# Summing the query squares together with the output squares of the gated DeltaNet heads, without a root and factors of their own

## What is computed

```
q_a = l2norm(q_a); k_a = l2norm(k_a)        # x * rsqrt(sum(x*x) + 1e-6), over the 128 of a head
q = q * dk ** -0.5
o = chunked gated delta rule(q, k, v, g, beta)
o_a = rms_norm(o_a, gdn_norm) * silu(z_a)   # o * rsqrt(mean(o*o) + 1e-6)
```

## Time and profile before

| | |
|---|---|
| median of three runs | 2443.24 us |
| span of the profiled execution, first to last instruction | 2435.2 us |
| what lies around the span (difference of the two) | 8.0 us |
| TensorE busy in the span | 2333.0 us (96%) |
| VectorE, ScalarE, GpSimd busy | 1191.3, 997.0, 1127.8 us |
| mean granted TensorE clock | 0.980 of full |
| one eight-tile pair | 88 us, six of them |

### The profile page before, as it was taken

The page is one execution under the profiler, slowest core; times in us unless marked ns, Lnnn a source line. Parts: engine busy times, 40 slices in busy tenths (PEclk is TensorE's granted clock), DMA queues, the critical chain, the costliest instruction groups (busy, mean ns, idle before and its releaser), DMA issues.

```text
span 2435.2 us, 30531 instructions
## 1 busy us (share of the span) xinstructions
PE 2333.0 (96%) x11700; PEld 1926.4 (79%) x11700; DVE 1191.3 (49%) x2356; ACT 997.0 (41%) x1925; POOL 1127.8 (46%) x824
## 2 busy tenths in 40 slices
PE   6999998999999999999989999989999999999997
PEld 5678887788878888888867888878887788888886
DVE  4677676644442344440147777675454423444302
ACT  5554444444542333332265355344555323333222
POOL 4364454344345555554443553552343555555542
PEclk9999999999999999999989999989999999999998
DMA  4211111122223333333322111101222333333332
GB/s 135 61 52 53 48 44 40 35 75 77 75 78 96 96 93 98 95 99 96 96 65 65 44 49 52 44 27 53 78 75 69 89 96 94 96 99 96 96 99 82
DMA packets 98497, 183.20 MB, mean 75 GB/s; under 512 B 10929, under 2 KB 11057, under 8 KB 98225
## 3 DMA queue, kind: packets, MB, share of 16 engines
q1 hardware_dynamic: 98352, 181.26, 26.2%
HBM read 179.12 MB, written 2.10 MB: 74 GB/s over the span
## 4 chain that ended last, share of the span: by engine, by line
PE 87%; DVE 7%; ACT 3%; issue 1%; POOL 0%; DMA 0%; SPq 0%; DVEq 0%; ACTq 0%
PE bank L1288 84%; PE bank L1354 2%; DVE conv_acc L834 1%; PE bank L1580 1%; ACT w_hi L505 1%; PE bank L1348 1%; DVE ob_lo L831 1%; DVE a_t L834 1%; DVE packed L1065 0%; DVE qk_t L834 0%; ACT oa_hi L516 0%; DMA vecs_all<-vecs 0%; DVE normalised L834 0%; DVE left L834 0%; DVE packed_rows L831 0%
## 5 line engine op out<-in xcount | busy, mean ns | idle before, releaser
L418 POOL TENSOR_TENSOR w_lo<-w_raw,w_hi 128x512 fp32r<-128x512 f32 x668 | 935.3, 1422 | 1206.8 <-ACT w_hi L505 1206.6
L1288 PE MATMUL bank<-xn_hi,w_hi 128*128 128x512 f32 x1936 | 784.2, 405 | 10.9 <-POOL w_lo L418 3.6
L1288 PE MATMUL bank<-xn_hi,w_lo 128*128 128x512 f32 x1936 | 784.2, 405 | 0.0
L1288 PE MATMUL bank<-xn_lo,w_hi 128*128 128x512 f32 x1936 | 779.7, 403 | 0.0
L505 ACT ACTIVATE w_hi<-w_raw 128x512 fp32r<-128x512 f32 x668 | 384.6, 623 | 739.5 <-PE bank L1288 733.4
L1288 PEld LDWEIGHTS bank<-xn_hi,w_hi 128*128 128x128 f32 x1936 | 369.2, 191 | 89.4 <-issue 8.5
L1288 PEld LDWEIGHTS bank<-xn_hi,w_lo 128*128 128x128 f32 x1936 | 369.9, 191 | 77.6 <-issue 7.3
L1288 PEld LDWEIGHTS bank<-xn_lo,w_hi 128*128 128x128 f32 x1936 | 369.1, 191 | 77.0 <-issue 4.1
L831 DVE TENSOR_TENSOR residual<-residual,bank 128x512 f32<-128x512 f32 x32 | 22.0, 686 | 259.4 <-PE bank L1288 259.2
L1288 PE MATMUL bank<-mid_hi,w_hi 128*128 128x512 f32 x352 | 136.9, 389 | 0.0
L1288 PE MATMUL bank<-mid_lo,w_hi 128*128 128x512 f32 x352 | 136.9, 389 | 0.0
(11 more groups left out here) (256 smaller groups left out, 3449.4 us busy)
## 6 DMA issues: line engine op xcount, KB each, us to landing
w_raw<-w_tiles SPq DMA_DIRECT2D x668, 256.0 KB, 2.6
residual<-x_t SPq DMA_DIRECT2D x4, 512.0 KB, 5.2
out_t<-normalised SPq DMA_DIRECT2D x8, 256.0 KB, 2.2
rope<-rope SPq DMA_DIRECT2D x1, 1024.0 KB, 10.0
mats<-mats SPq DMA_DIRECT2D x1, 704.0 KB, 7.6
vecs_all<-vecs SPq DMA_DIRECT2D x1, 133.0 KB, 7.5
```

What stands on the lines that cost most here:

```text
L418: nc.gpsimd.tensor_tensor(w_lo[j][:], w_raw[j][:], w_hi[j][:].bitcast(F32), ALU.subtract).then_inc(s_lo, 1)
L1288: return nc.tensor.matmul(out, lhsT, rhs, start=start, stop=stop)
```

## The change

The query squares are taken with a scale (sqrt(1e-6) times 128) and kept until the end of the pair; for that `sq_q` gets slots of its own, and two attention tiles move by 64 bytes. At the end VectorE adds them to the output squares (`om`), and the one chain of ones-products `oss` sums both. The stage `ss`, `varq`, the query's root, reciprocal, `fq`, `fq2`, `ox` and `orf` go. Since `ss` leaves `STAGES` and `FILL_WEIGHT`, the products of a pair are dealt out anew over the steps that are left, and for tile 0 the convolution's places are now written out by hand, too.

```diff
-        sq_q = per_head("sq_q", 5)
+        sq_q = per_head("sq_q", 18)
...
-        STAGES = (["kt", "gb", "ss", "vt", "kbT", "kk", "qk", "sub", "T0_"]
+        STAGES = (["kt", "gb", "vt", "kbT", "kk", "qk", "sub", "T0_"]
...
-        FILL_WEIGHT = {8: {"start": 4.5, "gb": 4, "ss": 1.5, "qk": 4.5, "sub": 7.3, "T0_": 0.5, "P3_": 0.6, "w": 0.8, "oss": 3},
-                       4: {"start": 4.5, "kt": 2, "gb": 4, "ss": 1.5, "qk": 4, "sub": 6, "w": 0.8, "oss": 3}}
+        FILL_WEIGHT = {8: {"start": 4.5, "gb": 4, "qk": 4.5, "sub": 7.3, "T0_": 0.5, "P3_": 0.6, "w": 0.8, "oss": 3},
+                       4: {"start": 4.5, "kt": 2, "gb": 4, "qk": 4, "sub": 6, "w": 0.8, "oss": 3}}
...
-                    spot = {1: ("kk", "kk", "qk", "sub", "T0_")}
+                    spot = {0: ("vt", "vt", "kbT", "kk", "kk"), 1: ("kk", "kk", "qk", "sub", "T0_")}
...
# ScalarE
-                    nc.scalar.activation(sq_q[s][:], q_f[s][:], ACT.Square)
+                    nc.scalar.activation(sq_q[s][:], q_f[s][:], ACT.Square, scale=EPS ** 0.5 * HD)
...
-                act.wait_ge(gdn_v.sem, gdn_v.after(t, "varq1"))
-                nc.scalar.activation(rinv[:, :, 0, :], rinv[:, :, 0, :], ACT.Sqrt)
...
# VectorE
-                for s in range(2):
-                    dve.wait_ge(gdn_p.sem, gdn_p.after(t, f"ss{s}"))
-                    V.tensor_scalar(rinv[:, s, 0, :], bz[s][:, :NC], 4 * EPS, None, ALU.add)
...
-                dve.wait_ge(gdn_a.sem, gdn_a.after(t, "sqrtq"))
-                V.reciprocal(rinv[:, :, 0, :], rinv[:, :, 0, :])
-                V.tensor_scalar(fq[:, 0], rinv[:, :, 0, :], HD ** -0.5, None, ALU.mult)
-                stt(fq[:, 1], fq[:, 0], 1.0 / HD, fq[:, 0], ALU.mult, ALU.mult)
...
                 for s in range(2):
+                    dve.wait_ge(gdn_a.sem, gdn_a.after(t, f"osq{s}"))
+                    tt_(o_sq[s][:], o_sq[s][:], sq_q[s][:], ALU.add).then_inc(gdn_v.step(f"om{s}"), 1)
+                for s in range(2):
                     dve.wait_ge(gdn_p.sem, gdn_p.after(t, f"oss{s}"))
-                    tt_(ocol[:, s, :], bx[s][:, :NC], fq[:, 1, s, :], ALU.mult)
-                V.tensor_scalar(ocol[:], ocol[:], EPS, None, ALU.add)
+                    V.tensor_scalar(ocol[:, s, :], bx[s][:, :NC], 1.0 / HD, 4 * EPS * EPS * HD, ALU.mult, ALU.add)
...
-                tt_(ocol[:], ocol[:], fq[:, 0], ALU.mult)
...
# TensorE
-                for s in range(2):
-                    pe.wait_ge(gdn_a.sem, gdn_a.after(t, f"sqq{s}"))
-                    for c in range(NC):
-                        last = mm(bz[s][:, c:c + 1], sq_q[s][:, c, :], ones[:, 0:1])
-                    last.then_inc(gdn_p.step(f"ss{s}"), 1)
-                d.issue(dense_after["ss"])
-
                 for s in range(2):
                     pe.wait_ge(front_v.sem, front_v.after(t, f"silu{4 * s}"))
-                    pe.wait_ge(gdn_v.sem, gdn_v.after(t, f"varq{s}"))
...
-                    pe.wait_ge(gdn_a.sem, gdn_a.after(t, f"osq{s}"))
+                    pe.wait_ge(gdn_v.sem, gdn_v.after(t, f"om{s}"))
```

More of the change, by code:

```diff
@@ L152, in hybrid_trunk @@
         fac = sb("fac", [2, 3, NC])
-        fq = sb("fq", [2, 2, NC])
         rinv = sb("rinv", [2, 2, NC])
@@ L223, in hybrid_trunk @@
                                       for j, n in enumerate(("dx0", "dxs", "dx1", "dxt", "rq", "rk")))
-        dv = sb("dv", [SEQ], at=slot(52))
-        d_tanh = sb("d_tanh", [SEQ], at=slot(53))
+        dv = sb("dv", [SEQ], at=slot(52) + 64)
+        d_tanh = sb("d_tanh", [SEQ], at=slot(53) + 64)
         sg0 = slot(14) + 64
@@ L327, in hybrid_trunk @@
         gdn_p = steps("gdn_pe", [m for st in STAGES for m in (["sub"] if st == "sub" else two(st))])
-        gdn_a = steps("gdn_act", two("ztanh", "sqq", "sqk") + ["sqrtk", "sqrtq"] + two("exp", "kbT", "eg", "T0_")
+        gdn_a = steps("gdn_act", two("ztanh", "sqq", "sqk") + ["sqrtk"] + two("exp", "kbT", "eg", "T0_")
                       + [m for L in LV for m in two(f"P{L}_", f"T{L}_")][:-2] + two("w", "osq", "o") + ["osqrt"])
-        gdn_v = steps("gdn_dve", ["hcol", "htot", "zact0", "zact1", "vark", "rinvk", "fac", "kb0", "kd0", "kb1", "kd1"] + two("varq", "ga", "vb")
-                      + ["rinvq", "fq", "fq2"] + two("at") + ["inv0", "red0", "red1", "row"] + two("qk") + [m for j in range(SB - 1) for m in (f"col{j}", f"inv{j + 1}")] + ["whole"] + two("i0_")
+        gdn_v = steps("gdn_dve", ["hcol", "htot", "zact0", "zact1", "vark", "rinvk", "fac", "kb0", "kd0", "kb1", "kd1"] + two("ga", "vb")
+                      + two("at") + ["inv0", "red0", "red1", "row"] + two("qk") + [m for j in range(SB - 1) for m in (f"col{j}", f"inv{j + 1}")] + ["whole"] + two("i0_")
                       + [m for L in LV for m in two(f"U{L}_")]
                       + [m for c in range(NC) for m in two(f"V{c}_", f"S{c}_")][:-2]
-                      + two("ox") + ["ovar", "orinv", "orf"] + two("ou", "og"))
+                      + two("om", "ovar") + ["orinv"] + two("ou", "og"))
         gdn_g = steps("gdn_pool", two("ds", "dg", "mt3_", "qd", "mt4_", "mt5_", "qm", "mt6_", "kbg"))
@@ L443, in mask @@
                         nc.gpsimd.tensor_tensor(mt[L % 2][s][:], a_t[s][:], mat4(M_LEVEL + L - FIRST), ALU.mult).then_inc(gdn_g.step(f"mt{L}_{s}"), 1)
-                stages("kt", "gb", "ss")
+                stages("kt", "gb")
                 for s in range(2):
@@ L622, in gdn @@
                     act.wait_ge(front_v.sem, front_v.after(t, f"silu{4 * s + 2}"))
-                    nc.scalar.activation(sq_q[s][:], q_f[s][:], ACT.Square).then_inc(gdn_a.step(f"sqq{s}"), 1)
+                    nc.scalar.activation(sq_q[s][:], q_f[s][:], ACT.Square, scale=EPS ** 0.5 * HD).then_inc(gdn_a.step(f"sqq{s}"), 1)
                 for s in range(2):
@@ L631, in gdn @@
                 stages("kt", "gb")
-                act.wait_ge(gdn_v.sem, gdn_v.after(t, "varq1"))
-                nc.scalar.activation(rinv[:, :, 0, :], rinv[:, :, 0, :], ACT.Sqrt).then_inc(gdn_a.step("sqrtq"), 1)
-                stages("ss")
                 for s in range(2):
@@ L669, in gdn @@
                 stages("oss")
-                act.wait_ge(gdn_v.sem, gdn_v.after(t, "ovar"))
+                act.wait_ge(gdn_v.sem, gdn_v.after(t, "ovar1"))
                 nc.scalar.activation(ocol[:], ocol[:], ACT.Sqrt).then_inc(gdn_a.step("osqrt"), 1)
@@ L1031, in gdn @@
                 for s in range(2):
-                    dve.wait_ge(gdn_p.sem, gdn_p.after(t, f"ss{s}"))
-                    V.tensor_scalar(rinv[:, s, 0, :], bz[s][:, :NC], 4 * EPS, None, ALU.add).then_inc(gdn_v.step(f"varq{s}"), 1)
-                for s in range(2):
                     dve.wait_ge(gdn_p.sem, gdn_p.after(t, f"gb{s}"))
@@ L1119, in gdn @@
                 for s in range(2):
+                    dve.wait_ge(gdn_a.sem, gdn_a.after(t, f"osq{s}"))
+                    tt_(o_sq[s][:], o_sq[s][:], sq_q[s][:], ALU.add).then_inc(gdn_v.step(f"om{s}"), 1)
+                for s in range(2):
                     dve.wait_ge(gdn_p.sem, gdn_p.after(t, f"oss{s}"))
-                    tt_(ocol[:, s, :], bx[s][:, :NC], fq[:, 1, s, :], ALU.mult).then_inc(gdn_v.step(f"ox{s}"), 1)
-                dve.wait_ge(gdn_v.sem, gdn_v.after(t, "ox1"))
-                V.tensor_scalar(ocol[:], ocol[:], EPS, None, ALU.add).then_inc(gdn_v.step("ovar"), 1)
+                    V.tensor_scalar(ocol[:, s, :], bx[s][:, :NC], 1.0 / HD, 4 * EPS * EPS * HD, ALU.mult, ALU.add).then_inc(gdn_v.step(f"ovar{s}"), 1)
                 stages("oss")
@@ L1126, in gdn @@
                 V.reciprocal(ocol[:], ocol[:]).then_inc(gdn_v.step("orinv"), 1)
-                dve.wait_ge(gdn_v.sem, gdn_v.after(t, "orinv"))
-                tt_(ocol[:], ocol[:], fq[:, 0], ALU.mult).then_inc(gdn_v.step("orf"), 1)
                 for s in range(2):
@@ L1556, in gdn @@
                     if s == 0:
-                        pe.wait_ge(gdn_v.sem, gdn_v.after(t, "orf"))
+                        pe.wait_ge(gdn_v.sem, gdn_v.after(t, "orinv"))
                     spread(by[s], ocol[:, s, :]).then_inc(gdn_p.step(f"obc{s}"), 1)
```

## The result

Before 2443.19 us, after **2454.15 us** median of four runs each beside one another (2442.96 to 2443.61, and 2449.73 to 2458.88); the ratio is 1.0052, interval 1.0035 to 1.0069. The change makes the kernel slower by about half a per cent. The forecast was 2459.4 with a range of 2441 to 2475. The runs of after lie in two groups: 2449.73 and 2449.81 us at a mean granted clock of 0.976, 2458.49 and 2458.88 at 0.973. The profiled execution is the longest of them (span 2456.8 for 2458.88 us). In every run, time and span differ by 2.0 to 2.1 us, so the 8.0 us taken ahead of the prediction for what lies around the span do not lie there: the span of 2435.2 belongs to an execution of before of some 2437.3 us. Beside the experiments before ran from 2434.92 to 2443.81 us, so that is one of its short executions.

What follows compares the result with a forecast made beforehand. TensorE is busy 96%, but VectorE, with ScalarE behind it, sets the pace from `sub` to `U3_`. Terms +10.8 (six pairs), +3.4 (clock at `kk`), +2.0 (4-tile pairs): +16.2 on span 2435.2, plus 8.0: 2459.4 us, range 2441 to 2475.

Steps and rivals of the forecast that it cites:

- Tile 1 one product too late, VectorE idle for what it saved: Ahead of `sub`: tile 1 ends at `qk`'s first product, so VectorE idles the 1.9 us it saved before `t0_1`.
- Wait at `sub` 3.7 us: TensorE's wait for `packed_rows` before `sub` in eight-tile pairs grows from 1.98 to 3.7 us as the trace counts it.
- The limit of 2.5: Sign against the forecast: it is wrong if the wait at `sub` stays under 2.5 us.
- pairs under 88: Sign against the forecast: it is wrong if the pairs take less than 88 us.
- the price of the fall after `sub`: Time lost when the clock falls after the wait at `sub`, in every pair: 1.7 us taken, 2.8 by the farthest row.
- Fall of the clock after it in two pairs, +3.4 us: After the new wait at `kk`: clock falls in two of six eight-tile pairs, 1.7 us each, bounds 0 to 10.2.
- The wait of 0.2: At `oss`, end of an eight-tile pair: TensorE waits 0.2 us for the squares of o and the new sums.
- Pairs with 4 tiles +1.0 each: `kk` starts at about 399.8, `inv` 0.9 us later, `sub` about 0.5 later, sums cost 0.4; bounds -1.5 and +2.5.
- the third rival: VectorE's new sums run slow beside a busy GpSimd: 14.4 us more, 2473.5 us; chance 0.08.
- the clock does not fall more than now: Rival: each eight-tile pair gives +0.1 us instead of +1.8, 4-tile pairs +2.0, total 2445.8 us; chance 0.15.
- TensorE's saving stays: Rival: 1.7 us come off in each of 8 pairs, 13.6 us, total 2429.6 us; chance 0.13.
- The added sums are slow: Rival: VectorE's sums before `oss`, slowed by GpSimd, end 1.0 and 1.8 us later; 2473.5 us; chance 0.08.

Runs made afterwards that it cites:

- run 2: The kernel before, norm as before, with only the new deal of the dense products (weight of `ss` 0, tile 0's places as in the change); 2455.28 us, ratio 1.0049.
- run 3: The changed kernel with VectorE's first operations of tile 1 (`t0_1`, `t1_1`) moved from `kk` to `qk`, behind `packed_rows`; 2438.62 us, ratio 0.9993.
- run 4: The changed kernel without VectorE's two sums (`om`), query squares left out of the output; 2448.27 us, ratio 1.0026.
- run 5: The changed kernel with four dense products of an eight-tile pair moved from behind `oss` to ahead of it; 2446.82 us, ratio 1.0026.
- run 6: The changed kernel with VectorE's operations of tile 2 all at `T0_`, before the subtraction of `U3_`; 2444.67 us, ratio 1.0018.
- run 8: The changed kernel with the old deal, more products ahead of `oss`, tile 1's first operations behind `packed_rows`, tiles 2 and 3 placed anew; 2414.33 us, ratio 0.9892.
- run 9: The kernel before, query norm as it was, with the places and deal of run 8; 2431.15 us, ratio 0.9964.
- run 1: The changed kernel with the old deal of the dense products (`gb` takes over the weight of `ss`, 4 to 5.5); 2438.36 us, ratio 0.9991.

## Why the prediction was right, and where it was off

The forecast, slower through a longer wait at `sub` and a clock that falls after it, is what happened, and runs 2 and 3 show it from both sides. That the number came within 5 us of the median owes something to luck, as said below. Step by step:

- *Tile 1 one product too late, VectorE idle for what it saved.* Right: 1.71 us idle for a predicted 1.9.
- *Wait at `sub` 3.7 us.* 3.13 to 3.17. From the start of VectorE's first operation on tile 1 to `sub` I took the 5.5 us of before; it is 241.28 - 236.28 = 5.0, since `inv`, moved in time, takes 0.55 us, where it took 1.10 before. The limit of 2.5 held. The other sign ("pairs under 88") did not hold everywhere: a pair without a fall takes 87.62.
- *`sub` to `U3_`: 10.76 us at full clock.* Measured 1375.94 - 1365.16 = 10.78 in the pair without a fall. With one it is 254.98 - 241.28 = 13.70.
- **The term that was mis-sized: the price of the fall after `sub`.** 1.7 us was taken, the nearest row, with 2.8 as the dear end, "in every pair". It cost 13.70 - 10.78 = 2.9 in four pairs, 1.4 in the one at 1452 (row below), and nothing in the one at 1365: 13.0 us in six, for a predicted 10.1. In runs 4 to 6 both sizes come, too: up to `U3_`, 1.4 to 1.6 us in nine pairs and 2.7 to 2.9 in six, and in three nothing.

```profile
1452.78:1464.97 12.19, 12.19 (x58) 9.60 (x58) 9.12 (x29) 4.30 (x8) 8.90 (x7) 0.88 0.16 44
```

- *Wait at `kk` 1.1.* 1.02; the releaser was `v_b`, not `kbT`. *Fall of the clock after it in two pairs, +3.4 us.* Wrong: in no eight-tile pair.
- *Wait behind `U3_` 1.0, the 97th product 3.15 us after `U3_`.* 0.89, and 258.04 - 254.98 = 3.06. *`P6_` 0.2:* 0.26. *`P4_` 0.25:* none.
- **The term that was left out: the clock after `oss`.** The wait of 0.2 was there (0.3), and I costed it at its own length. The fall behind it, some 1.6 us a pair where it comes (4.5 for both falls less 2.9, and run 3), is 6.4 us in four pairs, about what run 4 shows as the sums' 6 us.
- *Pairs with 4 tiles +1.0 each.* +2.1 and +2.5. `kk` came 3.0 us earlier, as the 399.8 said, but its group of 16 then ran at the low clock (3.75 us instead of 2.46), tile 0 came later, and `inv` began 2.7 us later than before instead of 0.9, at the end of the rotary chain that I had put ahead of it:

```profile
413.09 3.75 PE L1274 MATMUL bank<-kbT,k_f 128*128 128x128 f32 x16 [2.42 <-DVE v_b L830]
427.53 2.08 PE L1274 MATMUL bank<-packed_rows,mats 128*128 128x512 f32 x2 [5.94 <-DVE packed_rows L827]
```

**The total.** The sum of +16.2 us was for the span, and between the two profiles it is +21.6. In us, of the difference of 5.4 the fall at `sub` has +2.9, the one after `oss` +6.4, the missing fall at `kk` -3.4 and the pairs with 4 tiles +2.6; against them a pair without a fall came 0.3 shorter than 87.9 instead of 0.1 longer, about -2.2 in six: together +6.3. The forecast of 2459.4 then had the 8.0 us on top, where runs show 2.1. With 2.1 it is 2453.5, beside a median of 2454.15, and that agreement is chance as well: by the medians the change costs 11.0 us, and a sum of 16.2 fits only because it stands on a short execution of before. The 2473.5 of the third rival should read 2473.8.

Of the rivals, "the clock does not fall more than now" (2445.8) holds for one pair of six in the profiled execution. *TensorE's saving stays* needed `packed_rows` to move with TensorE; once it does (run 8 against run 9) the whole 13.6 us come off. *The added sums are slow* falls: 1.28 us for two, and all sixteen take 0.68 to 0.69 us each. In the first window above GpSimd works for 0.48 us, until 206.48, when the sums have just begun (206.45); their cost came through a wait, not through their length. Whether they would be slow beside a busy GpSimd no run here shows.

Open: the extra 3 us of run 6; what splits the four runs of after into two groups (only one of them was profiled); and why the clock sometimes does not fall after a wait of 3.1 us at `sub`. In the profiled executions of after and of runs 4, 5 and 6 that wait stands in 24 eight-tile pairs; in four of them no fall follows (the pair at 1365 here, one in run 5, two in run 6), and all four are the first pair of a layer.

## What to carry to other kernels

When a step leaves a schedule in which other work is dealt out by weights, the deal itself is a change: count what ends before which step, for a tile that ends one product later can hold a whole chain. An idle stretch of TensorE costs more than its length where the clock falls behind it, so the unit to compare is a whole period with its mean granted clock, and waits are best all brought down together, since taking one away may only move the fall. A removed piece of work is worth its time only if each engine's wait moves with it; measure it in a version where no wait stands in the way.

## What the runs showed of the hardware that was not expected

- The granted clock went from 1.00 to 0.50 (2.4 to 1.2 GHz) shortly after one-column products with a wait of only about 0.3 us before them (after and runs 1 and 3: in four eight-tile pairs of six, run 6: in three, with the same wait in the others), and in none of the eight-tile pairs of before and of runs 4, 5 and 8, where the one-column products are the same and the wait is absent. A wait of 0.50 us in the same place in the pairs with 4 tiles brought none in after and in runs 1, 3 and 6.
- Waits of 0.7 to 1.3 us with full-width products between them (runs 3, 8, 9) brought no fall in the stretch up to `U3_`; waits of 1.9 us were followed by one in some pairs and not in others, and those of 3.12 to 3.17 us by one in 20 pairs of 24 (after and runs 4, 5, 6). The same wait in the same place is not a sure sign.
- The prices of a fall as measured: from `sub` to `U3_` 1.4 to 1.6 us in some pairs and 2.7 to 2.9 in others, after `oss` 1.6 us. With the clock at 1.00 throughout, equal pairs agree within 0.1 us (84.19, 84.24, 84.27).
